# Tile 1's cross attention moved into the waits of tile 0's chain: scores in its own half of `y`, low parts on GpSimd

## The chip, the cores and the metric

The kernel runs on one core of one Trainium2 chip. The metric is the device time of one execution in microseconds (us), the median of several runs. Times inside the program come from one profiled execution and count from its first instruction.

## The reference, cut to what matters

One decoder layer over 256 tokens of 1024 channels, in float32: self attention (dilated and block-sparse), then cross attention to 256 memory rows, then the PEER expert layer, then a last norm. The change lies in the cross attention; what follows it is the expert layer.

```
x = x + cross_attention(rmsnorm(x), rmsnorm(mem))   # 4 heads of 128 channels
    lg = q @ k.T / sqrt(128); p = softmax(lg); o = p @ v; return o @ w_o
x = x + peer(rmsnorm(x))                            # 8 heads, per token:
    q = h @ w_q; sc = q @ sub_keys.T                # 2 x 128 key scores a head
    top 16 of each side, top 16 of the sums -> 16 experts and softmax gates
    y = sum over 128 experts of gate * gelu(u[e] . h) * v[e]
y = rmsnorm(x)
```

## The kernel before, in words

The 256 tokens are two tiles of 128 (`t` = 0 and 1). Every engine has its own instruction stream in an order that is written out by hand; semaphores join the streams. A matmul product goes into one of four PSUM banks `ps` in turn. `product_order` lists the products; the place in that list gives the bank (place modulo 4) and the counts that engines wait for, so the product that is four places behind waits until the first is taken out. `taken["act"]` and `taken["dve"]` count what ScalarE and VectorE have taken. The second PSUM tensor, `y` (two tiles by 1024 columns, the other four banks), collects the residual, the cross output and then the expert sum of each tile; `start_output(t, half)` puts `x` into it with an identity product.

Products in float32 quality are made of three in `fp32r`: each operand is split into a high part (a cast, on ScalarE) and a low part (value minus high part). `split_panel` does that for weight panels: ScalarE the high part, VectorE the low part. Activations of the cross output are `o_hi`, `o_lo`, those of the expert queries `h_hi`, `h_lo`.

Cross attention, tile by tile: `cross_score` (TensorE), `cross_bound` (VectorE, minimum of the negated scores), `cross_exp` (ScalarE), `cross_probs` (VectorE, normalises), `cross_turn` (TensorE transposes) and its copy (ScalarE), `cross_attend` (TensorE, two heads `i` at a time), `take_cross_o` (ScalarE, high part), `cross_o_low` (VectorE, low part), `cross_output` (TensorE, 24 products of 128x512 into `y`). Then for each tile `gained_rows` (VectorE, times the gain), `turn_rows` (TensorE), high and low part of the turned rows, `query_product` of head 0, `query_turn`, `query_scores`, and on VectorE `route_first`, which finds the first 16 experts of tile 0. Before the change tile 1's scores, exponentials and normalisations stand between tile 0's steps in all four streams.

The expert layer is 256 gathers ("slots"): 16 units (8 heads x 2 tiles) of 16 experts a token. Each is an indirect DMA of 128 rows of 8 KB, issued by GpSimd (`issue`, L1756) into one of 16 buffers (11 at first). The first waits for the first eight experts of tile 0; the second (`OWN_PLACE_OVER`) also for the last product of `cross_output(1)`; the sixth for `gained_rows(1)`; others for tile 1's query products; from the twelfth on for a buffer that TensorE has given back (`slot_free`). VectorE makes the dot product of a slot (L1644), ScalarE gelu, weight and a diagonal matrix, TensorE adds the row into `y` (L851).

SyncE loads the weight panels, 1 MB each. After `qpeer1` its stream waits until `cross_o1_1` (tile 1, heads 2 and 3) is produced; only then it loads `qpeer7` into a buffer over the cross attention's tensors, and behind it `qpeer3` and `qpeer4`.

Of the kernel before, what the change touches and what calls it, by code (L numbers as in the profile page):

```python
# [7 lines left out]
ALU = mybir.AluOpType  # L8
# [6 lines left out]
P = 128  # L15
D = 1024
S = 256
# [139 lines left out]
def product_order():  # L157
# [57 lines left out]
    def turned_rows(t):  # L215
        for half in range(2):
            if t == 0:
                add(f"cross_probs_t{half}_1", "act")
            add(f"turn{t}_{half}", "both")
# [49 lines left out]
def build(nc, x_in, mem_in, rel_bias, panels, keys_in, experts, gain_cols, gain_rows, ident_in,  # L269
          onehot_in, mask_in, iota_in, out):  # L270
    with ExitStack() as ctx:
# [191 lines left out]
        c_exp_ready = sem("c_exp_ready")  # L463
# [48 lines left out]
        def merged(c):  # L512

            return gates[:, c:c + 2, :]

# [70 lines left out]
        def _(pe):  # L586
# [156 lines left out]
            def cross_score(h, t):  # L743

                b = begin(f"cross_score{h}_{t}")
                pe.matmul(b[:, 0:S], qcT[:, h, t * P:(t + 1) * P], ckT[:, h, :],
                          start=True, stop=True).then_inc(product_ready, 1)

# [9 lines left out]

            def cross_attend(i, t):

                b = begin(f"cross_o{i}_{t}")
                all_taken(f"cross_probs_t{i}_{t}")
                for k in range(2):
                    for m in range(TILES):
                        mm = pe.matmul(b[:, k * P:(k + 1) * P], cV[:, m, (2 * i + k) * P:(2 * i + k + 1) * P],
                                       c_probsT[:, i, k * S + m * P:k * S + (m + 1) * P],
                                       start=(m == 0), stop=(m == TILES - 1))
                mm.then_inc(product_ready, 1)
# [12 lines left out]
            cross_score(2, 1)  # L781
            cross_score(3, 1)

            def cross_output(t):

                for j in range(2):
                    w_high, w_low = panel(f"ocross{j}")
                    dst = y[:, t, j * 512:(j + 1) * 512]
                    for k in range(CROSS_HEADS):
                        if j == 0 and k % 2 == 0:  # L790
                            all_taken(f"cross_o{k // 2}_{t}")
                        o_high, o_low = cut(o, slice(None), k, slice(t * P, (t + 1) * P))
# [6 lines left out]
            def turn_rows(t):  # L799

                for half in range(2):
                    if t == 0:
                        cross_turn(half, 1)
# [5 lines left out]
                    mm.then_inc(product_ready, 1)  # L809

# [104 lines left out]
        def _(act):  # L915
# [150 lines left out]
            def cross_exp(h, t):  # L1066

                b = take(f"cross_score{h}_{t}")
                act.wait_ge(c_neg_ready, t * CROSS_HEADS + h + 1)
                took(nc.scalar.activation(c_probs[:, h, t * S:(t + 1) * S], b[:, 0:S], ACT.Exp,  # L1070
                                          bias=c_neg[:, h, t:t + 1], scale=-1.0, accum_out=c_sum[:, h, t:t + 1]))
# [32 lines left out]
            def turned_rows(t):  # L1104

                for half in range(2):
                    b = take(f"turn{t}_{half}")
                    nc.scalar.copy(h_hi[:, 4 * half:4 * half + 4, t * P:(t + 1) * P],
                                   b.rearrange("p (k c) -> p k c", k=4)).then_inc(high_ready, 1)
# [14 lines left out]
            for half in range(2):  # L1124
# [74 lines left out]
            turned_rows(1)  # L1199
# [69 lines left out]
        def _(dve):  # L1269
# [134 lines left out]
            def cross_bound(h, t):  # L1404

                b = take(f"cross_score{h}_{t}")
                nc.vector.tensor_reduce(c_neg[:, h, t:t + 1], b[:, 0:S], AX.X, ALU.min).then_inc(c_neg_ready, 1)

            def cross_probs(h, t):

                dve.wait_ge(taken["act"], taken_count(f"cross_score{h}_{t}"))
# [6 lines left out]
            def cross_o_low(i, t):  # L1418

                b = take(f"cross_o{i}_{t}")  # L1420
                dve.wait_ge(high_ready, high_count(f"cross_o{i}_{t}"))
# [19 lines left out]
            for h in range(1, CROSS_HEADS):  # L1441
                cross_probs(h, 1)
# [457 lines left out]
```

## Time and profile before

| | us |
|---|---|
| median of 3 runs | 964.17 (963.46 to 964.51) |
| the profiled execution's own time | 961.84 |
| its span, first to last instruction | 960.0 |

The span is what the rows below divide up. The profiled execution is 2.3 us below the median of the runs, so differences in the span are carried over to the median as they are. TensorE is busy for 84% of the span, VectorE 65%, ScalarE 43%, GpSimd 36%; the GpSimd queue's gathers carry 268.45 MB of the 324.88 MB that the DMA engines move.

### The profile page before, as it was taken

What the parts mean: (1) busy time and instruction counts of PE and PEld (TensorE: products, weight loads), DVE (VectorE), ACT (ScalarE), POOL (GpSimd) and SP (SyncE); (2) the same over time, 40 slices, a digit from 0 to 9 for tenths busy, and PEclk for the clock granted to TensorE, in tenths of its full rate; (3) what the DMA queues carried; (4) which work ended last, traced back from release to release, by engine and by line L of the source; (5) the groups of instructions that cost most, each with busy time, mean ns of one, the idle gap of its engine ahead of it and who ended that gap; (6) DMA issues with size and microseconds to landing.
All of it is one profiled execution on the core that took longest, in us unless ns stands there. A gap on an engine that the chain in (4) does not pass through costs nothing.

```text
span 960.0 us, 11578 instructions
## 1 busy us (share of the span) xinstructions
PE 808.6 (84%) x3620; PEld 506.1 (53%) x3620; DVE 620.0 (65%) x1446; ACT 410.4 (43%) x1006; POOL 347.5 (36%) x301
## 2 busy tenths in 40 slices
PE   5999999999997899998987777777777777776776
PEld 5999998799976545553553232222222222222232
DVE  5433686465557786878777666676666766665554
ACT  5444565543564456434534324233242432424243
POOL 0000065040003455556546434444444444444410
PEclk9999999999999999999999999999999999999989
DMA  6998433257316999999999999999999999999994
GB/s 248 269 213 209 172 131 132 89 220 280 138 44 235 417 419 422 421 422 421 421 421 421 423 421 422 421 422 423 421 422 422 422 422 422 422 423 420 422 423 203
DMA packets 48803, 324.88 MB, mean 338 GB/s; under 512 B 5508, under 2 KB 8824, under 8 KB 10104
## 3 DMA queue, kind: packets, MB, share of 16 engines
q0 software_dynamic: 36864, 268.45, 67.3%
q1 hardware_dynamic: 11752, 55.61, 17.4%
q8 instruction: 25, 0.41, 0.2%
q10 hardware_dynamic: 144, 0.26, 0.1%
q14 instruction: 18, 0.15, 0.0%
HBM read 322.77 MB, written 1.54 MB: 338 GB/s over the span
## 4 chain that ended last, share of the span: by engine, by line
DMA 47%; PE 35%; DVE 6%; ACT 5%; issue 5%; POOL 1%; DVEq 0%; SPq 0%; ACTq 0%; POOLq 0%
DMA late_ring<-in_experts,expert 44%; PE y L851 8%; PE ps L603 7%; PE ps L604 7%; PE ps L605 7%; DMA arena<-in_experts,expert 2%; DVE w_lo L1284 2%; ACT w_hi L928 1%; ACT diag L1155 1%; PE ps L703 1%; POOL late_ring L1756 1%; ACT acts L1148 1%; PE ps L691 1%; DMA raw<-in_panels 1%; PE ps L681 1%
## 5 line engine op out<-in xcount | busy, mean ns | idle before, releaser
L851 PE MATMUL y<-late_ring,diag 128*128 128x512 f32 x504 | 238.7, 608 | 64.8 <-ACT diag L1155 64.8
L851 PE MATMUL y<-arena,diag 128*128 128x512 f32 x504 | 236.8, 605 | 59.7 <-ACT diag L1155 59.7
L1756 POOL DMA_INDIRECT arena<-in_experts,expert x127 | 154.4, 1216 | 231.9 <-PE y L851 117.7
L1644 DVE CUSTOM_DVE_ANT_0 arena<-arena 128x1024 f32<-128x1024 f32 x127 | 155.5, 1225 | 99.5 <-DMA arena<-in_experts,expert 99.1
L1644 DVE CUSTOM_DVE_ANT_0 late_ring<-late_ring,arena 128x1024 f32<-128x1024 f32 x129 | 157.9, 1224 | 88.8 <-DMA late_ring<-in_experts,expert 88.3
L1756 POOL DMA_INDIRECT late_ring<-in_experts,expert x129 | 150.2, 1164 | 165.8 <-PE y L851 139.9
L851 PEld LDWEIGHTS y<-late_ring,diag 128*128 128x128 f32 x504 | 91.8, 191 | 199.6 <-ACT diag L1155 105.8
L851 PEld LDWEIGHTS y<-arena,diag 128*128 128x128 f32 x504 | 92.1, 191 | 194.6 <-ACT diag L1155 99.1
L1140 ACT ACTIVATE acts<-dots 128x2 f32<-128x2 f32 x126 | 25.6, 203 | 335.1 <-DVE dots L1644 335.1
L1284 DVE TENSOR_TENSOR w_lo<-raw,w_hi 128x2048 fp32r<-128x2048 f32 x40 | 94.0, 2353 | 77.3 <-ACT w_hi L928 77.3
L603 PE MATMUL ps<-h_hi,w_hi 128*128 128x256 f32 x400 | 116.8, 292 | 1.7 <-DVE h_lo L1316 1.7
L604 PE MATMUL ps<-h_lo,w_hi 128*128 128x256 f32 x400 | 113.8, 284 | 0.0
L605 PE MATMUL ps<-h_hi,w_lo 128*128 128x256 f32 x400 | 113.7, 284 | 0.0
L928 ACT CAST w_hi<-raw 128x2048 fp32r<-128x2048 f32 x40 | 76.2, 1904 | 50.3 <-DMA raw<-in_panels 33.4
L1155 ACT ACTIVATE diag<-ident,acts 128x128 f32<-128x128 f32 x252 | 87.4, 394 | 12.1 <-PE y L851 3.1
L603 PEld LDWEIGHTS ps<-h_hi,w_hi 128*128 128x128 f32 x400 | 77.3, 193 | 5.6 <-issue 3.2
L604 PEld LDWEIGHTS ps<-h_lo,w_hi 128*128 128x128 f32 x400 | 77.4, 194 | 1.2 <-issue 1.2
L605 PEld LDWEIGHTS ps<-h_hi,w_lo 128*128 128x128 f32 x400 | 77.4, 193 | 0.0
L1736 POOL TENSOR_SCALAR arena<-arena,row_inv 128x128 f32<-128x128 f32 (+3 forms) x24 | 25.7, 1085 | 137.1 <-DVE row_inv L1338 136.8
L1148 ACT ACTIVATE acts<-acts,gate 128x1 f32<-128x1 f32 x252 | 60.5, 287 | 4.1
L603 PE MATMUL ps<-w_hi,h_hi 128*128 128x256 f32 x160 | 46.9, 293 | 2.1 <-DVE h_lo L1457 1.3
L604 PE MATMUL ps<-w_lo,h_hi 128*128 128x256 f32 x160 | 46.1, 288 | 0.0
(238 smaller groups left out, 992.5 us busy)
## 6 DMA issues: line engine op xcount, KB each, us to landing
raw<-in_panels SPq DMA_DIRECT2D x41, 1024.0 KB, 5.0
arena<-in_panels SPq DMA_DIRECT2D x5, 1024.0 KB, 6.7
arena<-line_scratch SPq DMA_DIRECT2D x8, 320.0 KB, 10.0
late_ring<-in_experts,expert POOLq DMA_INDIRECT x129, 31.7
arena<-in_experts,expert POOLq DMA_INDIRECT x127, 31.7
x<-in_x SPq DMA_DIRECT2D x2, 512.0 KB, 3.9
arena<-in_mem SPq DMA_DIRECT2D x1, 1024.0 KB, 7.3
out<-x SPq DMA_DIRECT2D x3, 256.0 KB, 7.1
```

Source lines behind the costliest of these rows:

```text
L603: pe.matmul(dst, stationary[0], moving[0], start=first, stop=False)
L604: pe.matmul(dst, stationary[0], moving[1], start=False, stop=False)
L605: return pe.matmul(dst, stationary[1], moving[0], start=False, stop=last)
L851: mm = pe.matmul(y[:, t, half * 512:(half + 1) * 512], diag[:, s % DIAGS, :], row[:, at:at + 512], start=False, stop=False, skip_group_che ...
L928: nc.scalar.copy(split_parts(n)[0], raw_panel(n)).then_inc(w_hi_ready, 1)
L1140: nc.scalar.activation(acts[:, g * GROUP:(g + 1) * GROUP], dots[:, g * GROUP:(g + 1) * GROUP], ACT.Gelu).then_inc(acts_ready, 1)
L1148: i = nc.scalar.activation(acts[:, s:s + 1], acts[:, s:s + 1], ACT.Copy, scale=gate_now[:, s:s + 1])
L1155: i = nc.scalar.activation(diag[:, s % DIAGS, :], ident[:], ACT.Copy, scale=acts[:, s:s + 1])
L1284: nc.vector.tensor_tensor(low, raw_panel(n), high.bitcast(F32), ALU.subtract).then_inc(w_lo_ready, 1)
L1644: i = nc.vector.tensor_tensor_reduce(row, row, h_rows[:, t, :], 1.0, 0.0, ALU.mult, ALU.add, dots[:, s:s + 1])
L1736: i = nc.gpsimd.tensor_scalar(pr, pr, row_inv[:, r, t:t + 1], None, ALU.mult)
L1756: nc.gpsimd.indirect_dma_start(out=slot(u, s), out_offset=None, in_=experts, in_offset=bass.IndirectOffsetOnAxis(ap=expert[:, parity, s:s ...
```

## The change

Tile 1's four score products are written straight into `y[:, 1]` (its own two banks, empty at this point) instead of `ps`. Two of them go ahead of tile 0's scores, two between tile 0's probability transposes; `start_output(0, 0)` moves behind tile 0's scores. Their minimum is taken by two VectorE instructions of two heads each, behind tile 0's low parts; their four exponentials stand on ScalarE behind `take_cross_o` of tile 0; the four normalisations stand on VectorE between the halves of tile 0's `gained_rows`. Tile 1's transposes are moved behind tile 0's turned rows, on ScalarE behind both turned halves and both squares; its heads are attended between `query_product(0, 0)`, `query_turn` and `query_scores` of tile 0. ScalarE now copies each pair of tile 1's attended heads twice (high part, and a plain copy into SBUF), and GpSimd makes the low part from the two. `cross_output(1)` waits for these, and so does the first gather.

```
     for h in range(CROSS_HEADS):
         add(f"cross_score{h}_0", "act")
-    add("cross_score0_1", "act")
     for i in range(2):
         add(f"cross_probs_t{i}_0", "act")
-    add("cross_o0_0", "both")
-    add("cross_score1_1", "act")
-    add("cross_o1_0", "both")
-    add("cross_score2_1", "act")
-    add("cross_score3_1", "act")
+    for i in range(2):
+        add(f"cross_o{i}_0", "both")
...
     cross_output(0)
     turned_rows(0)
-    add("cross_o0_1", "both")
     add("qpeer0_0", "act")
-    add("cross_o1_1", "both")
     add("qturn0_0", "act")
+    add("cross_o0_1", "act")
     add("key_score0_0", "act")
+    add("cross_o1_1", "act")
     cross_output(1)
...
-            start_output(0, 0)
+            all_taken("qcross0")
+            late_score(0)
+            late_score(1)
             all_taken("qcross1")
             for h in range(CROSS_HEADS):
-                cross_score(h, 0)
+                cross_score(h)
+            start_output(0, 0)
             start_output(0, 1)
-            cross_score(0, 1)
             cross_turn(0, 0)
+            late_score(2)
+            late_score(3)
             cross_turn(1, 0)
             cross_attend(0, 0)
-            cross_score(1, 1)
             cross_attend(1, 0)
-            cross_score(2, 1)
-            cross_score(3, 1)
...
             cross_output(0)
             turn_rows(0)
-            cross_attend(0, 1)
+            query_product(0, 0)
+            b = begin("cross_o0_1")
+            all_taken("cross_probs_t0_1")
+            cross_head(b, 0, 0)
+            query_turn(0, 0)
+            cross_head(b, 0, 1).then_inc(product_ready, 1)
+            query_scores(0, 0)
+            cross_attend(1, 1)
+            pe.wait_ge(late_exp_ready, CROSS_HEADS)
             start_output(1, 0)
-            query_product(0, 0)
-            cross_attend(1, 1)
-            query_turn(0, 0)
             start_output(1, 1)
-            query_scores(0, 0)
             cross_output(1)
...
             for h in range(CROSS_HEADS):
-                cross_exp(h, 0)
-            cross_exp(0, 1)
-            take_cross_turn(0, 0)
-            take_cross_turn(1, 0)
-            cross_exp(1, 1)
-            take_cross_o(0, 0)
-            take_cross_o(1, 0)
-            cross_exp(2, 1)
-            cross_exp(3, 1)
+                b = take(f"cross_score{h}_0")
+                act.wait_ge(c_neg_ready, h + 1)
+                took(cross_exp(h, 0, b[:, 0:S]))
+            for i in range(2):
+                take_cross_turn(i, 0)
+            for i in range(2):
+                take_cross_o(i, 0)
+            for h in range(CROSS_HEADS):
+                act.wait_ge(c_neg_ready, CROSS_HEADS + h // 2 + 1)
+                cross_exp(h, 1, late_scores(h, 1)).then_inc(late_exp_ready, 1)
             load_sqrt_table()
...
-            for half in range(2):
-                take_cross_turn(half, 1)
-                rows_square(0, half)
-            turned_rows(0)
-            take_cross_o(0, 1)
+            rows_square(0, 0)
+            turned_half(0, 0)
+            turned_half(0, 1)
+            rows_square(0, 1)
+            for i in range(2):
+                take_cross_turn(i, 1)
             rows_root(0)
             split_panel(PANELS.index("qpeer1"))
...
             take_query_tile(0, 0)
-            take_cross_o(1, 1)
             take_turned_query(0, 0)
+            late_o_high(0)
             take_scores_tile(0, 0)
+            late_o_high(1)
             scale_rows(0)
...
-            gained_rows(0)
+            gained_half(0, 0)
+            for h in range(CROSS_HEADS):
+                cross_probs(h, 1)
+            gained_half(0, 1)
             turned_rows(0)
-            cross_o_low(0, 1)
             rows_mean(0)
             rows_rstd(0)
             split_panel(PANELS.index("qpeer1"))
-            cross_o_low(1, 1)
...
+            for i in range(2):
+                pool.wait_ge(taken["act"], taken_count(f"cross_o{i}_1"))
+                pool.wait_ge(late_o_out, i + 1)
+                nc.gpsimd.tensor_tensor(o_lo[:, 2 * i:2 * i + 2, P:S], late_o(i),
+                                        o_hi[:, 2 * i:2 * i + 2, P:S].bitcast(F32), ALU.subtract
+                                        ).then_inc(late_o_ready, 1)
```

New helpers that these lines call:

```
        def late_scores(h, n):
            return y[:, 1, h * S:(h + n) * S]
            def late_score(h):
                pe.matmul(late_scores(h, 1), qcT[:, h, P:S], ckT[:, h, :],
                          start=True, stop=True).then_inc(late_scores_ready, 1)
            def late_o_high(i):
                b = take(f"cross_o{i}_1")[:, 0:S].rearrange("p (k c) -> p k c", k=2)
                nc.scalar.copy(o_hi[:, 2 * i:2 * i + 2, P:S], b).then_inc(late_o_out, 1)
                took(nc.scalar.copy(late_o(i), b))
            def late_bound(i):
                dve.wait_ge(late_scores_ready, 2 * i + 2)
                nc.vector.tensor_reduce(c_neg[:, 2 * i:2 * i + 2, 1], late_scores(2 * i, 2).rearrange(
                    "p (h m) -> p h m", h=2), AX.X, ALU.min).then_inc(c_neg_ready, 1)
```

## Rows read from the trace of the kernel before

**Rows 1.** Windows: stretch, length, busy us by engine, granted clock, DMA share, GB/s.

```profile
293.50:301.00 7.50, 7.33 (x39) 6.29 (x40) 5.20 (x37) 3.42 (x3) 0.00 (x0) 1.00 0.98 415
301.00:305.00 4.00, 1.78 (x15) 1.58 (x14) 3.66 (x10) 0.37 (x1) 1.51 (x2) 1.00 0.01 2
400.00:944.00 544.00, 425.76 (x1054) 181.01 (x1052) 367.87 (x952) 203.75 (x629) 251.78 (x215) 0.99 1.01 422
```

**Rows 2.** GpSimd's timeline: start, length, instruction; in brackets the idle time before it.

```profile
303.18 1.24 POOL L1756 DMA_INDIRECT arena<-in_experts,expert  x1 [86.54 <-DVE expert L1620]
...
338.08 0.94 POOL L1756 DMA_INDIRECT arena<-in_experts,expert  x1 [3.38 <-PE y L851]
```

**Rows 3.** SyncE's timeline, the load behind `cross_o1_1`.

```profile
291.97 0.33 SPq L555 DMA_DIRECT2D arena<-in_panels  x1
```

**Rows 4.** TensorE's timeline, tile 0's attention and its first output product.

```profile
273.41 0.63 PE L755 MATMUL ps<-ident,arena 128*128 128x128 f32 x4 [0.96 <-DVE arena L1415]
...
275.44 1.05 PE L765 MATMUL ps<-arena 128*128 128x128 f32 x8
...
277.91 0.58 PE L794 MATMUL y<-w_hi,o_hi 128*128 128x512 f32 x1
```

**Rows 5.** ScalarE's timeline in the same stretch, and its table load.

```profile
276.16 0.47 ACT L1070 ACTIVATE arena<-ps,c_neg 128x256 f32<-128x256 f32 x1 [1.50 <-DVE c_neg L1407]
...
276.62 0.64 ACT L1081 CAST o_hi<-ps 128x256 fp32r<-128x256 f32 x2
...
279.64 1.28 ACT L964 ACT_TABLE_LOAD   x1
```

**Rows 6.** VectorE's timeline: low parts, two of the normalisations, the second gained half.

```profile
277.08 0.76 DVE L1423 TENSOR_TENSOR o_lo<-ps,o_hi 128x256 fp32r<-128x256 f32 x2 [1.02 <-ACT o_hi L1081]
...
279.53 0.35 DVE L1415 TENSOR_SCALAR arena<-arena,c_inv 128x256 f32<-128x256 f32 x1
...
279.99 0.35 DVE L1415 TENSOR_SCALAR arena<-arena,c_inv 128x256 f32<-128x256 f32 x1
...
283.84 0.69 DVE L1449 TENSOR_TENSOR arena<-y,arena 128x512 f32<-128x512 f32 x1 [2.04 <-PE y L796]
```

**Rows 7.** TensorE's timeline from tile 0's turned rows to its key scores.

```profile
283.64 0.60 PE L755 MATMUL ps<-ident,arena 128*128 128x128 f32 x4
...
287.94 0.36 PE L603 MATMUL ps<-w_hi,h_hi 128*128 128x256 f32 x1 [0.63 <-DVE h_lo L1457]
...
290.89 1.05 PE L765 MATMUL ps<-arena 128*128 128x128 f32 x8
...
293.67 0.68 PE L835 MATMUL ps<-keysT,qpT 128*128 128x128 f32 x4 [0.66 <-DVE o_lo L1423]
```

**Rows 8.** ScalarE's timeline in that stretch: turned rows, the high part of `qpeer1`.

```profile
286.39 1.09 ACT L1108 CAST h_hi<-ps 128x512 fp32r<-128x512 f32 x2
...
288.98 1.89 ACT L928 CAST w_hi<-raw 128x2048 fp32r<-128x2048 f32 x1
```

**Rows 9.** VectorE's timeline: low part of `qpeer1`, start of `route_first`, first experts.

```profile
290.90 2.29 DVE L1284 TENSOR_TENSOR w_lo<-raw,w_hi 128x2048 fp32r<-128x2048 f32 x1 [1.63 <-ACT w_hi L928]
...
294.90 0.30 DVE L1586 MAX8 ranked<-arena 128x8 f32<-128x128 f32 x1 [1.37 <-ACT arena L1175]
...
302.72 0.17 DVE L1620 CAST expert<-expert_f 128x8 uint32<-128x8 f32 x1
```

**Rows 10.** VectorE's timeline earlier, a weight split while GpSimd computes.

```profile
212.07 3.42 DVE L1284 TENSOR_TENSOR w_lo<-raw,w_hi 128x2048 fp32r<-128x2048 f32 x1 [3.87 <-ACT w_hi L928]
```

**Rows 11.** GpSimd's groups by shape: busy us, mean ns of one.

```profile
L1751 POOL TENSOR_TENSOR o_lo<-arena,o_hi 128x512 fp32r<-128x512 f32 x4 | 7.1, 1808 | 0.0
```

**Rows 12.** TensorE's longest pause in this stage, its timeline.

```profile
306.15 0.41 PE L827 MATMUL ps<-ident,qpT 128*128 128x128 f32 x2 [3.37 <-DVE arena L1449]
```

**Rows 13.** Windows of the granted clock, before and after that pause; columns as in Rows 1.

```profile
273.40:277.90 4.50, 3.85 (x26) 3.17 (x27) 1.24 (x4) 2.22 (x7) 0.00 (x0) 1.00 0.00 0
308.00:314.00 6.00, 5.29 (x25) 4.92 (x24) 2.86 (x8) 3.56 (x9) 4.76 (x5) 0.50 0.98 380
```

More of the change, by code:

```diff
@@ L216, in turned_rows @@
         for half in range(2):
+            add(f"turn{t}_{half}", "both")
             if t == 0:
                 add(f"cross_probs_t{half}_1", "act")
-            add(f"turn{t}_{half}", "both")
     def query(h, t):
@@ L462, in build @@
         c_neg_ready = sem("c_neg_ready")
-        c_exp_ready = sem("c_exp_ready")
+        late_scores_ready = sem("late_scores_ready")
+        late_exp_ready = sem("late_exp_ready")
+        late_o_out = sem("late_o_out")
+        late_o_ready = sem("late_o_ready")
         c_inv_ready = sem("c_inv_ready")
@@ L757, in cross_turn, with cross_head @@
                 mm.then_inc(product_ready, 1)
+            def cross_head(b, i, k):
+                for m in range(TILES):
+                    mm = pe.matmul(b[:, k * P:(k + 1) * P], cV[:, m, (2 * i + k) * P:(2 * i + k + 1) * P],
+                                   c_probsT[:, i, k * S + m * P:k * S + (m + 1) * P],
+                                   start=(m == 0), stop=(m == TILES - 1))
+                return mm
             def cross_attend(i, t):
@@ L762, in cross_attend @@
                 all_taken(f"cross_probs_t{i}_{t}")
[L763 to L768, printed above, removed]
-            start_output(0, 0)
+                cross_head(b, i, 0)
+                cross_head(b, i, 1).then_inc(product_ready, 1)
+            all_taken("qcross0")
+            late_score(0)
+            late_score(1)
             all_taken("qcross1")
             for h in range(CROSS_HEADS):
-                cross_score(h, 0)
+                cross_score(h)
+            start_output(0, 0)
             start_output(0, 1)
-            cross_score(0, 1)
             cross_turn(0, 0)
+            late_score(2)
+            late_score(3)
             cross_turn(1, 0)
             cross_attend(0, 0)
-            cross_score(1, 1)
             cross_attend(1, 0)
-            cross_score(2, 1)
-            cross_score(3, 1)
             def cross_output(t):
@@ L809, in turn_rows @@
                     mm.then_inc(product_ready, 1)
+                    if t == 0:
+                        cross_turn(half, 1)
             def query_product(h, t):
@@ L1064, in _, with cross_exp @@
             take_queries(1)
[L1066 to L1071, printed above, removed]
+            def cross_exp(h, t, b):
+                return nc.scalar.activation(c_probs[:, h, t * S:(t + 1) * S], b, ACT.Exp,
+                                            bias=c_neg[:, h, t:t + 1], scale=-1.0, accum_out=c_sum[:, h, t:t + 1])
             def take_cross_turn(i, t):
@@ L1102, in rows_square, with turned_half @@
                                      ).then_inc(ffn_sq_ready, 1)
-            def turned_rows(t):
-                for half in range(2):
-                    b = take(f"turn{t}_{half}")
-                    nc.scalar.copy(h_hi[:, 4 * half:4 * half + 4, t * P:(t + 1) * P],
-                                   b.rearrange("p (k c) -> p k c", k=4)).then_inc(high_ready, 1)
+            def turned_half(t, half):
+                b = take(f"turn{t}_{half}")
+                nc.scalar.copy(h_hi[:, 4 * half:4 * half + 4, t * P:(t + 1) * P],
+                               b.rearrange("p (k c) -> p k c", k=4)).then_inc(high_ready, 1)
             def rows_root(t):
@@ L1122, in scale_rows @@
                                      ).then_inc(h_rows_ready, 1)
-            for half in range(2):
-                take_cross_turn(half, 1)
-                rows_square(0, half)
-            turned_rows(0)
-            take_cross_o(0, 1)
+            rows_square(0, 0)
[4 more added lines that the diff above has]
+                take_cross_turn(i, 1)
             rows_root(0)
@@ L1198, in _ @@
             take_scores_tile(1, 0)
-            turned_rows(1)
+            for half in range(2):
+                turned_half(1, half)
             rows_root(1)
@@ L1667, in _ @@
             route_first()
-            gained_rows(1)
+            for half in range(2):
+                gained_half(1, half)
             split_panel(PANELS.index("qpeer2"))
@@ L1753, in _ @@
                                         ).then_inc(merged_ready, 1)
+            for i in range(2):
+                pool.wait_ge(taken["act"], taken_count(f"cross_o{i}_1"))
[3 more added lines that the diff above has]
+                                        ).then_inc(late_o_ready, 1)
             def issue(u, s, parity):
```

65 lines of the change are left out of this document (32 added, 33 removed).

## The prediction

> **What bounds the kernel now.** I read the windows first. From 400 to 944 us the DMA engines are fully busy at 422 GB/s; a gather is 128 rows of 8 KB, 1.05 MB, so one takes 2.49 us and 256 of them 636 us. Ahead of that lies a hole: from 293.50 to 301.00 three weight panels load at 415 GB/s, then for 4.00 us the DMA engines move 2 GB/s [rows 1]. The hole ends when the first gather's data starts to flow, about 1.8 us after its issue at 303.18, and that issue had waited for VectorE's first experts [rows 2]. So the end of the kernel is the start of the gathers plus a fixed transfer time. The busy shares mislead: TensorE's 84% decides nothing behind 305 us. What decides is the serial chain that leads to 303.18, and I walked it backwards in the four engines' timelines, looking in each step for tile 1's work standing between two of tile 0's.
>
> The chain has three places with such work. (1) Tile 0's attended heads are ready on TensorE, but ScalarE sits in tile 1's exponential, which itself waited 1.50 us for a minimum on VectorE; the high parts start only at 276.62 [rows 5], the low parts at 277.08 [rows 6], the first output product at 277.91 [rows 4]. (2) From 283.64 to 287.94 TensorE has tile 1's transposes ahead of tile 0's rows, and ScalarE puts two copies and two squares ahead of the turned rows' high parts, which start at 286.39 [rows 7, 8]. (3) From 287.94 to 294.90, where `route_first` begins, the query product is followed by tile 1's attention at 290.89, and the key scores wait until 293.67 for a bank that VectorE frees with tile 1's low part, behind the split of `qpeer1` [rows 7, 9].
>
> **The change, place by place.** Up to 273.41, where tile 0's second pair of transposes starts [rows 4], nothing moves: two late scores replace one `start_output` in front of the scores (two products of 256 columns for one of 512), and tile 0's minima, exponentials and normalisations wait on each other, not on tile 1's minimum that went. The other two late scores fit into the 0.96 us for which TensorE waits there [rows 4].
>
> Place 1. Transposes at 273.41 are ready 0.63 later [rows 4], ScalarE's copy takes 0.6 more (as one of the two casts of 128x512 in [rows 8]), so the second pair is attended from 274.73 and ready 1.05 later, 275.78. The first pair, attended from 273.85, has its high part at 275.3 and its low part at 275.75, each about 0.4 [rows 5, 6]. The first output product starts at 275.8 instead of 277.91. The second pair's low part is there at 276.65, needed six products later, at 277.2. Gain 2.1.
>
> Place 2. The output's products take 283.64 - 277.91 = 5.7 [rows 4, 7], so tile 0's first turned rows are issued at 281.5. Ready after 0.6, high part 0.6, low part 0.7 (the 128x512 of [rows 6]), and TensorE starts the query product at 283.6 with 0.15 of semaphore time. Before: 287.94 [rows 7]. Gain of this place 2.2, sum 4.3. Two covers must hold. ScalarE has tile 1's four exponentials (0.47 each, behind two minima of about 0.6 each: 277.3 to 279.2) and the table load of 1.28 with its dummy (to 280.8) and a square of 0.6 (to 281.4) [rows 5]; the turned rows come at 282.1, so 0.7 is free. VectorE has four normalisations of 0.46 (the distance of the two in [rows 6]) behind the first gained half, 279.5 to 281.4; the second gained half can start at 283.84 - 2.1 = 281.7 [rows 6], so 0.3 is free. If that cover is gone, what is late next is the second turned half, which the query product needs only 12 products in, so a few tenths more cost nothing.
>
> Place 3. The query product takes 290.89 - 287.94 = 2.95 [rows 7] and is ready at 286.7. ScalarE is not: after the second high part (283.6) come a square of 0.6, two copies of 0.5 and the root (285.3), and then the high part of `qpeer1`, 1.89 [rows 8], of which the next instruction waits 1.8. The query is copied at 287.1, not 286.7: 0.4 lost. Copy 0.37, transpose 0.4, copy 0.37, with 0.1 between each: key scores start at 288.5, the bank being free. From key scores to `route_first` it is 294.90 - 293.67 = 1.23 [rows 7, 9], so `route_first` starts at 289.75. VectorE's split of `qpeer1` follows ScalarE's at 287.2 and takes 2.29 [rows 9]: done at 289.5, just in time. The one head of tile 1 between the transposes is 0.44 on TensorE, which waits there anyway; the two extra ScalarE copies (0.3 each) fit between 288.45 and 289.2, where ScalarE would wait for the key scores. Gain of this place 0.8.
>
> Sum: 2.1 + 2.2 + 0.8 = 5.1, that is 294.90 to 289.75. `route_first` itself is unchanged (294.90 to the experts at 302.72 [rows 9]), so the first gather is issued at 298.0 and its data flows at 299.85.
>
> **What must come along.** The panels: SyncE's load at 291.97 waits for `cross_o1_1` [rows 3]. Attended from 288.95, that is ready at 290.0, so the loads run 1.8 earlier, to 299.2 [rows 1], 0.6 before the gathers. Were they later, their rest would only share the DMA engines, microsecond for microsecond; this caps the gain at 4.0 + 1.8 = 5.8. The low parts on GpSimd: 128x512 took 1.81 [rows 11], so 128x256 about 0.9; the second runs from 290.6 to 291.5. `cross_output(1)` starts at 291.6 (attention, then two `start_output` of 0.87) and needs it at 293.0; its 5.7 end at 297.3. The second gather waits for this and is wanted by 300.5. The first gather's new wait is over at 291.5. Behind that, tile 1's rows follow `route_first` on VectorE and so move by the same 5. If they did not: the sixteenth gather, issued at 338.08 [rows 2], has 15 gathers of 2.49 ahead of it, 305.0 + 37.3 = 342.3 at the least, and needs 1.8; that leaves 2.4, so an unmoved tile 1 would take back 2.7 at most.
>
> The price that the trace doesn't show is what GpSimd's subtraction does to VectorE in the selection. Bounds: nothing, or what a split lost while GpSimd computed, 3.42 - 2.29 = 1.13 [rows 9, 10]. Twice that is the upper end, 2.3. I take nothing: the splits have two tensors in SBUF, the instructions at 289.5 to 291.5 (maxima, replacements, index searches on 128x128) have one. A gain below zero cost can't come from here. The Trainium skill, page "SBUF — State Buffer", section "SBUF: two separate sides", says that a VectorE instruction with two SBUF inputs and a GpSimd one exclude each other for a whole instruction, and whoever came first holds the ports. The 3.42 agrees with it. By that rule the split of `qpeer1` holds the first subtraction until 289.5 and the second ends before the first sum of pairs in `route_first`, so the sum stays 5.1.
>
> **Rivals.** (a) GpSimd holds VectorE. For: [rows 10]. Against: the form of the instructions. One hit of 1.13 gives 4.0, two give 2.8: 960.2 to 961.4. (b) The panel loads do not move, because something keeps `cross_o1_1` at 291.8; then they end at 301.0, 1.15 after the gathers want to start, and the gain is 4.0: 960.2. Against: nothing of tile 1 but its copied transposes is in its way. (c) Slower: TensorE's clock falls inside the chain. After its pause of 3.37 us the granted clock was 0.50, that is 1.2 GHz, from 308 to 314 [rows 12, 13]. Tile 0's output (5.7) and query product (2.95) at that level cost 8.7 more, against 5.1 gained: 3.6 slower, 967.8. It decides from 5.1 us of matmul time at the low level. Against: with 3.85 of 4.50 busy and a pause of 0.96 the clock stayed at 1.00 [rows 4, 13], and the new order has no pause over 1 us in the chain. (d) The second gather waits for tile 1's output: it takes over 3.2 us of lateness (297.3 to 300.5) before it costs, 8.3 before all is lost. Then the time is that of before, 964.2.
>
> **How the numbers follow.** All differences are of the profiled span (960.0, its execution 961.84); the median of the runs, 964.17, is taken to move by the same amount: 964.17 - 5.15 = 959.0. Chances: forecast (gain 4.4 to 6) 0.72, (a) 0.12, (b) 0.07, (c) 0.04, (d) or another pace that takes nearly all back 0.05. The range goes down to the cap of 5.8 with 0.4 of scatter of the runs, 957.9, and up to one hit of (a) or (b) with the same scatter and something of a second, 960.9. What a measurement can tell from no change is 0.2%, 1.9 us: faster 0.91, same 0.05, slower 0.04.
>
> **What would show it.** First output product near 275.8, query product near 283.6, `route_first` near 289.7, first gather near 298.0; panel loads ending just before the gathers' data; DMA share 1.0 from there on, without a hole near 300 or 320 to 335. An exponential or table load directly ahead of the turned rows' high parts would break place 2; a longer split of `qpeer1` or longer maxima beside GpSimd's two subtractions would be (a). The prediction is wrong if the gathers start earlier by 5 and the end doesn't follow.

## The result, and the profile after

| | before | after |
|---|---|---|
| median of 5 runs, us | 963.46 (960.74 to 964.51) | 957.20 (956.54 to 959.27) |
| span of the profiled execution | 960.0 | 955.3 |

The ratio is 0.994, with a 95% interval of 0.9921 to 0.9958: the change is faster, by 6 us on these runs. The profiled spans differ by 4.7, of which 0.3 lies ahead of the changed stage (269.22 and 268.89 in the table below). The forecast was 959.0 in a range of 957.9 to 960.9, so the median lies 0.7 below the range. The chain is almost where it was foretold; what was off is told behind the experiments.

TensorE's timeline of the changed kernel, with the lines that answer to [rows 4] and [rows 7] (start, length, instruction, idle time before it):

```profile
273.08 0.63 PE L767 MATMUL ps<-ident,arena 128*128 128x128 f32 x4
273.54 2.01 PE L774 MATMUL ps<-arena 128*128 128x128 f32 x16
275.68 0.47 PE L813 MATMUL y<-w_hi,o_hi 128*128 128x512 f32 x1
...
281.28 0.60 PE L825 MATMUL ps<-ident,arena 128*128 128x128 f32 x4
...
283.44 0.36 PE L610 MATMUL ps<-w_hi,h_hi 128*128 128x256 f32 x1
...
286.39 0.60 PE L774 MATMUL ps<-arena 128*128 128x128 f32 x4
287.38 0.41 PE L846 MATMUL ps<-ident,qpT 128*128 128x128 f32 x2 [0.39 <-ACT qpT L1191]
...
288.30 0.68 PE L854 MATMUL ps<-keysT,qpT 128*128 128x128 f32 x4
```

Both pairs of heads now run in one piece (x16), and the first output product follows 2.6 us behind the start of tile 0's second pair of transposes, where it was 4.5. The first turned rows follow the output's last product directly (L825 at 281.28), and the key scores have no wait for a bank.

ScalarE's timeline, answering to [rows 5] and [rows 8]:

```profile
275.60 0.37 ACT L1102 CAST o_hi<-ps 128x256 fp32r<-128x256 f32 x1 [0.58 <-PE ps L774]
277.13 0.48 ACT L1091 ACTIVATE arena<-y,c_neg 128x256 f32<-128x256 f32 x1 [1.16 <-DVE c_neg L1442]
...
279.08 1.28 ACT L987 ACT_TABLE_LOAD   x1
...
281.91 0.59 ACT L1135 CAST h_hi<-ps 128x512 fp32r<-128x512 f32 x1 [0.76 <-PE ps L825]
...
285.09 1.92 ACT L951 CAST w_hi<-raw 128x2048 fp32r<-128x2048 f32 x1
286.88 0.40 ACT L1191 COPY qpT<-ps 128x256 f32<-128x256 f32 x1
```

Tile 1's exponential again waits over a microsecond for its minimum, but nothing of tile 0 stands behind it any more. The turned rows find ScalarE idle for 0.76 us: the cover of place 2 held. The query's copy has no idle time ahead of it: it came straight from the split of `qpeer1`, as foretold.

VectorE's timeline, answering to [rows 6] and [rows 9]:

```profile
276.07 0.42 DVE L1462 TENSOR_TENSOR o_lo<-ps,o_hi 128x256 fp32r<-128x256 f32 x1 [0.54 <-ACT o_hi L1102]
...
281.48 0.69 DVE L1482 TENSOR_TENSOR arena<-y,arena 128x512 f32<-128x512 f32 x1 [0.20 <-PE y L815]
...
287.04 2.29 DVE L1314 TENSOR_TENSOR w_lo<-raw,w_hi 128x2048 fp32r<-128x2048 f32 x1 [1.62 <-ACT w_hi L951]
289.53 0.30 DVE L1620 MAX8 ranked<-arena 128x8 f32<-128x128 f32 x1 [0.19 <-ACT arena L1203]
...
297.35 0.17 DVE L1654 CAST expert<-expert_f 128x8 uint32<-128x8 f32 x1
```

Here the covers (the time that VectorE still waits when the work put in front is done) were as thin as estimated, 0.20 us at the second gained half and 0.19 at `route_first`. The selection from 289.53 to 297.35 takes 7.82, exactly as before (294.90 to 302.72, [rows 9]), with both GpSimd subtractions near it. In the two kernels of the experiments that have no such subtraction it takes 7.82 and 7.80. So the price that I had put between 0 and 2.3 is 0, and the subtractions took 0.92 and 0.73:

```profile
289.00 0.92 POOL L1793 TENSOR_TENSOR o_lo<-arena,o_hi 128x256 fp32r<-128x256 f32 x1 [72.69 <-ACT arena L1109]
290.64 0.73 POOL L1793 TENSOR_TENSOR o_lo<-arena,o_hi 128x256 fp32r<-128x256 f32 x1 [0.72 <-ACT arena L1109]
298.45 1.21 POOL L1798 DMA_INDIRECT arena<-in_experts,expert  x1 [7.08 <-DVE expert L1654]
```

That is GpSimd's timeline, answering to [rows 2]. Its last line holds a surprise: the gather starts 1.10 us behind the start of the experts' line on VectorE, 298.45 - 297.35. Before, it was 0.46, 303.18 - 302.72 [rows 2, 9]. SyncE's load, answering to [rows 3], and the windows (stretch, length, busy us by engine, granted clock, DMA share, GB/s), answering to [rows 1]:

```profile
289.90 0.33 SPq L562 DMA_DIRECT2D arena<-in_panels  x1
```

```profile
291.50:299.10 7.60, 7.60 (x43) 6.53 (x42) 6.68 (x35) 2.01 (x2) 0.65 (x1) 1.00 0.97 405
299.10:300.30 1.20, 0.93 (x8) 0.72 (x7) 1.17 (x4) 0.24 (x1) 0.90 (x2) 1.00 0.02 7
308.00:314.00 6.00, 5.71 (x47) 5.31 (x46) 5.25 (x16) 2.86 (x7) 5.09 (x4) 1.00 1.01 419
400.00:940.00 540.00, 423.80 (x1040) 180.63 (x1039) 364.51 (x947) 200.07 (x621) 253.50 (x213) 0.98 1.01 422
```

The hole of 4.00 us ahead of the gathers has shrunk to 1.2, the rate behind it is the same 422 GB/s, and TensorE's clock, at 0.50 from 308 to 314 before [rows 13], is at 1.00 there. That is not where the gain comes from: from the first gather to the end it is 656.8 us with the low clock and 656.9 without it (next table).

### The profile page after: what moved, and what is told of

It is laid out like the page before. It is cut to its first block, busy times and chain, and to the rows that moved or that the text cites. A ratio compares the mean times of both kernels' runs of the same rounds, so it can differ in the third digit from the quotient of the medians.

```text
span 955.3 us, 11577 instructions
## 1 busy us (share of the span) xinstructions
PE 810.4 (85%) x3620; PEld 506.7 (53%) x3620; DVE 619.5 (65%) x1442; ACT 411.5 (43%) x1008; POOL 359.5 (38%) x303
## 4 chain that ended last, share of the span: by engine, by line
DMA 47%; PE 39%; issue 5%; ACT 4%; DVE 3%; POOL 1%; DVEq 0%; SPq 0%; ACTq 0%; POOLq 0%
DMA late_ring<-in_experts,expert 44%; PE y L870 9%; PE ps L610 8%; PE ps L611 8%; PE ps L612 8%; DMA arena<-in_experts,expert 2%; ACT diag L1183 1%; POOL late_ring L1798 1%; PE ps L710 1%; PE ps L698 1%; ACT acts L1176 1%; DMA raw<-in_panels 1%; DVE w_lo L1314 1%; PE ps L688 1%; ACT w_hi L951 1%
## 5 line engine op out<-in xcount | busy, mean ns | idle before, releaser
L870 PE MATMUL y<-late_ring,diag 128*128 128x512 f32 x504 | 241.2, 614 | 63.5 <-ACT diag L1183 63.5
L870 PE MATMUL y<-arena,diag 128*128 128x512 f32 x504 | 239.5, 611 | 58.9 <-ACT diag L1183 58.9
L1798 POOL DMA_INDIRECT late_ring<-in_experts,expert x129 | 155.0, 1202 | 161.3 <-PE y L870 135.4
L1798 POOL DMA_INDIRECT arena<-in_experts,expert x127 | 156.5, 1233 | 150.0 <-PE y L870 111.2
L1771 POOL TENSOR_SCALAR arena<-arena,row_inv 128x128 f32<-128x128 f32 (+3 forms) x24 | 29.1, 1227 | 133.4 <-DVE row_inv L1368 133.2
```

The costliest lines, as they stand in the source:

```text
L870: mm = pe.matmul(y[:, t, half * 512:(half + 1) * 512], diag[:, s % DIAGS, :], row[:, at:at + 512], start=False, stop=False, skip_group_che ...
L1771: i = nc.gpsimd.tensor_scalar(pr, pr, row_inv[:, r, t:t + 1], None, ALU.mult)
L1798: nc.gpsimd.indirect_dma_start(out=slot(u, s), out_offset=None, in_=experts, in_offset=bass.IndirectOffsetOnAxis(ap=expert[:, parity, s:s ...
```

## The experiments

All ratios are against the kernel before, from 6 to 12 executions of each kernel (5 in the row "after"). The runs e1 to e4, e5 to e8, and e9 with e10 are three comparisons, each with its own executions of the kernel before (25, 29 and 11); the changed kernel itself was timed only for the result and in e1. The table puts the profiled executions side by side. "Stage start" is the start of tile 0's first minimum, the first VectorE instruction behind the weight splits. Ahead of it the kernels differ in TensorE's first instructions for this stage, which cost the same (0.87 us of one `start_output` before, 0.86 of two late scores after), and e9 in the place of one panel load. "Experts" is the start of VectorE's last instruction for the first eight experts. All in us.

| kernel | stage start | from it to `route_first` | experts to first gather | first gather to end | span | ratio (95%) |
|---|---|---|---|---|---|---|
| before | 269.22 | 25.68 | 0.46 | 656.8 | 960.0 | 1 |
| after | 268.89 | 20.64 | 1.10 | 656.9 | 955.3 | 0.9940 (0.9921 to 0.9958) |
| e1 after again | 267.34 | 20.66 | 1.10 | 656.7 | 953.6 | 0.9951 (0.9938 to 0.9963) |
| e2 scores only | 269.22 | 23.63 | 0.46 | 656.8 | 957.9 | 0.9984 (0.9971 to 0.9996) |
| e3 rows behind | 270.59 | 22.45 | 1.10 | 656.7 | 958.7 | 0.9968 (0.9953 to 0.9982) |
| e4 low on VectorE | 270.28 | 21.85 | 0.46 | 657.2 | 957.6 | 0.9967 (0.9953 to 0.9980) |
| e5 wait apart | 269.59 | 20.64 | 0.47 | 657.0 | 955.5 | 0.9948 (0.9931 to 0.9964) |
| e6 delay ahead | 271.18 | 23.77 | 1.10 | 657.5 | 961.7 | 0.9996 (0.9981 to 1.0011) |
| e7 delay behind | 269.21 | 20.67 | 1.10 | 657.8 | 956.6 | 0.9974 (0.9962 to 0.9987) |
| e8 loads late | 269.12 | 20.66 | 1.11 | 662.8 | 961.5 | 1.0008 (0.9994 to 1.0021) |
| e9 apart, loads | 269.00 | 20.63 | 0.46 | 657.1 | 955.0 | 0.9951 (0.9935 to 0.9968) |
| e10 apart, once more | 271.50 | 20.63 | 0.46 | 656.5 | 956.9 | 0.9939 (0.9921 to 0.9957) |

### The changed kernel again

No edit. 

> The changed kernel once more, for its size and its scatter. Theory (the end follows the first gather one for one): first output product of tile 0 about 2.1 us, route_first about 5.1 us earlier than in the profile of before, the first gather 4.7 to 5.2 earlier, ratio 0.9940 to 0.9955. Rival (part of the 6.3 us between the two medians is not in this chain but in the scatter of executions): the ratio stays below 0.9940 only if the runs of before scatter upward again, and the profiled chain still shows about 5.

Ratio 0.9951: 4.7 us (5.3 between the medians), where the first comparison had 5.8 by its ratio and 6.3 between its medians. The first gather, counted from the stage start, is 4.4 us earlier than before, not the expected 4.7 to 5.2. The rival is borne out: part of the 6.3 was scatter of executions, and the profiled chain to `route_first` still shows 5.0. The median of the kernel before was 963.24 here, from 25 executions between 960.26 and 965.83. The chain repeated itself to 0.02 us (20.64 and 20.66), while the stage start moved by 1.55. So the gain of the change is stable, and the scatter that these profiles show comes from ahead of the stage. VectorE's timeline shows where. Before the change, the start of the weight split near 128 us and of the first minimum:

```profile
128.41 2.29 DVE L1284 TENSOR_TENSOR w_lo<-raw,w_hi 128x2048 fp32r<-128x2048 f32 x1
```

```profile
269.22 0.42 DVE L1407 TENSOR_REDUCE c_neg<-ps 128x1 f32<-128x256 f32 x1 [0.23 <-PE ps L746]
```

The same two instructions in this run:

```profile
126.51 2.29 DVE L1314 TENSOR_TENSOR w_lo<-raw,w_hi 128x2048 fp32r<-128x2048 f32 x1
```

```profile
267.34 0.42 DVE L1437 TENSOR_REDUCE c_neg<-ps 128x1 f32<-128x256 f32 x1
```

1.90 us early at 128 us, 1.88 early at the stage start: in this pair the difference was complete in the first 129 us, and nothing was added in the 140 us behind. Up to there the splits wait for weight panels (at 105.87 ScalarE's half of one waited 3.67 us for its load in this run). In the run with a delay ahead of `route_first` (below) that split starts at 130.37, 1.96 late, and the stage start is 1.96 late. In eleven of the twelve profiles the distance between the two instructions is 140.8 to 141.0 us; in the first profile of the changed kernel it is 140.0 (128.91 to 268.89).

### Place 1 alone

```
 kernel: as after, but
                 for half in range(2):
+                    if t == 0:
+                        cross_turn(half, 1)
                     b = begin(f"turn{t}_{half}")
...
-                    if t == 0:
-                        cross_turn(half, 1)
...
             cross_output(0)
             turn_rows(0)
-            query_product(0, 0)
-            b = begin("cross_o0_1")
-            all_taken("cross_probs_t0_1")
-            cross_head(b, 0, 0)
-            query_turn(0, 0)
-            cross_head(b, 0, 1).then_inc(product_ready, 1)
-            query_scores(0, 0)
-            cross_attend(1, 1)
+            cross_attend(0, 1)
             pe.wait_ge(late_exp_ready, CROSS_HEADS)
             start_output(1, 0)
+            query_product(0, 0)
+            cross_attend(1, 1)
+            query_turn(0, 0)
             start_output(1, 1)
+            query_scores(0, 0)
 ScalarE: copies, squares, high parts in the order of before
 VectorE: cross_o_low(0, 1) and cross_o_low(1, 1) where they were
 GpSimd: no subtractions
```

> Only the scores, exponentials and normalisations of tile 1 moved (place 1 of the prediction); transposes, attention and low parts where they were, low parts on VectorE. Theory: 2.1 us of gain, all of it there when tile 0's first output product starts, the rest of the chain as long as before: ratio 0.9978. Rival (the places are not additive, what place 1 gives is taken back by a later wait): the query product of tile 0 starts at the time of before, ratio 0.999 to 1.000.

From stage start to `route_first` 23.63 instead of 25.68: 2.05 of gain, all kept. TensorE's timeline has the query product here:

```profile
285.89 0.36 PE L610 MATMUL ps<-w_hi,h_hi 128*128 128x256 f32 x1 [0.62 <-DVE h_lo L1483]
```

at the same stage start (269.22) as before, where it was at 287.94 [rows 7]. The ratio, 0.9984, gives 1.5, with an interval from 0.4 to 2.8. The rival, a time of 0.999 to 1.000, is not excluded by the ratio alone; its sign in the profile, a query product at the time of before, is absent.

### Place 2 undone

```
-            rows_square(0, 0)
-            turned_half(0, 0)
-            turned_half(0, 1)
-            rows_square(0, 1)
-            for i in range(2):
-                take_cross_turn(i, 1)
+            for half in range(2):
+                take_cross_turn(half, 1)
+                rows_square(0, half)
+            for half in range(2):
+                turned_half(0, half)
 TensorE and product_order: cross_turn(half, 1) ahead of each turned half
```

> The changed kernel with place 2 undone: tile 1's transposes ahead of tile 0's turned rows on TensorE, two copies and both squares ahead of the high parts on ScalarE. Theory: 2.2 us of the gain go, first gather about 2.2 later than in the changed kernel, ratio about 0.997. Rival (these instructions lie in waits of ScalarE either way): first gather within 0.5 us of the changed kernel's, ratio 0.9945.

`route_first` comes at 22.45 instead of 20.64, 1.8 later; the ratio 0.9968 is 1.6 us above the changed kernel's. ScalarE's timeline shows the queue that was put back:

```profile
283.63 0.59 ACT L1097 COPY arena<-ps 128x512 f32<-128x512 f32 x1 [1.36 <-PE ps L767]
284.11 0.60 ACT L1128 ACTIVATE x<-y 128x512 f32<-128x512 f32 x1
...
284.69 0.59 ACT L1097 COPY arena<-ps 128x512 f32<-128x512 f32 x1
285.16 0.62 ACT L1128 ACTIVATE x<-y 128x512 f32<-128x512 f32 x1
...
285.74 1.09 ACT L1135 CAST h_hi<-ps 128x512 fp32r<-128x512 f32 x2
```

The query product is 2.15 later than in the changed kernel (16.70 behind the stage start against 14.55), the key scores only 1.81 (21.22 against 19.41). Most of the missing 0.34 is the time for which the query's copy waits behind ScalarE's half of the split of `qpeer1` in the changed kernel (it starts 3.44 behind the query product's start, here 3.14): places 2 and 3 are not quite additive. The rival, a first gather within 0.5 us, is out: it came 1.8 later, counted from the stage start.

### Low parts back on VectorE

```
-                nc.scalar.copy(o_hi[:, 2 * i:2 * i + 2, P:S], b).then_inc(late_o_out, 1)
-                took(nc.scalar.copy(late_o(i), b))
+                nc.scalar.copy(o_hi[:, 2 * i:2 * i + 2, P:S], b).then_inc(high_ready, 1)
...
             split_panel(PANELS.index("qpeer1"))
+            cross_o_low(0, 1)
+            cross_o_low(1, 1)
...
 GpSimd: no subtractions, no wait for them
```

> The changed kernel with tile 1's low parts on VectorE again, between the low part of qpeer1 and route_first, and without the second copies on ScalarE and the two subtractions on GpSimd. Theory: the second low part is ready only at about 290.3 and holds route_first to 290.7 instead of 289.5: 1.2 us of the gain go, ratio about 0.9955 to 0.9965. Rival (GpSimd's subtractions and the doubled copies cost what they save): no loss, ratio 0.9945 or lower.

VectorE's timeline:

```profile
290.65 0.42 DVE L1459 TENSOR_TENSOR o_lo<-ps,o_hi 128x256 fp32r<-128x256 f32 x1
291.79 0.42 DVE L1459 TENSOR_TENSOR o_lo<-ps,o_hi 128x256 fp32r<-128x256 f32 x1 [0.72 <-ACT o_hi L1106]
292.13 0.28 DVE L1619 MAX8 ranked<-arena 128x8 f32<-128x128 f32 x1
```

The second low part waits for ScalarE and holds `route_first` back by 1.21 (21.85 against 20.64), as expected. But the first gather follows the experts by 0.46 again, so only 0.6 of the 1.2 reaches it. Moving the low parts to GpSimd is worth 1.2 at `route_first`, and its form costs 0.64. Counted from the stage start the profile ends 0.9 to 1.0 later than the two of the changed kernel; the ratio, 0.9967, lies just above what was expected and can't tell 0.6 from 1.2.

### The first gather's wait apart

```
                     if n == 0:
-                        pool.wait_ge(late_o_ready, 2)
+                        wait_apart(pool, late_o_ready, 2)     # the wait on an instruction of its own
                         pool.wait_ge(first_experts_ready, 1)
```

> The changed kernel with one edit: the first gather's new wait for the low parts gets an instruction of its own ahead of it, so that the gather itself holds only the wait for the first experts, as before the change. Seen so far: from the experts on VectorE to the first gather on GpSimd 0.46 us in the three kernels without the new wait and 1.10 in the three with it. Theory (the wait for the experts stands in an instruction of its own when the gather has two waits, and the gather's start-up follows it): 0.46 again, first gather and end 0.6 earlier, ratio 0.9944 where the changed kernel has 0.9951. Rival (GpSimd pays this because it has computed shortly before): 1.10 stays, ratio 0.9951.

GpSimd's timeline, with the experts on VectorE at 298.03:

```profile
291.34 0.73 POOL L1793 TENSOR_TENSOR o_lo<-arena,o_hi 128x256 fp32r<-128x256 f32 x1 [0.72 <-ACT arena L1109]
298.50 1.25 POOL L1798 DMA_INDIRECT arena<-in_experts,expert  x1 [6.42 <-DVE expert L1654]
```

0.47, with GpSimd's subtractions still there: it is the form of the wait, not that GpSimd has computed. The trace has a separate semaphore instruction in both kernels. In the changed one it holds the wait for the experts and stands 0.9 us ahead of the gather, which itself holds the wait for the low parts, long over; here it is the other way round: the separate instruction, for the low parts, stands 6.4 us ahead of the gather. The same came out in two further runs, 0.46 each. Counted from the stage start, the three profiled executions with the wait apart end after 685.9, 686.0 and 685.4, the two of the changed kernel after 686.4 and 686.3. The ratios (0.9948, 0.9951, 0.9939) don't separate them from 0.9951 and 0.9940: the timed runs cannot show half a microsecond. That the 0.64 reaches the end rests on these five profiles alone.

### A delay ahead of `route_first`, and one behind it

```
+            for n in range(3):
+                nc.vector.tensor_reduce(idle[:, n:n + 1], g_ffn_row, AX.X, ALU.max)
             route_first()
```

and the same lines behind `route_first()`.

> The changed kernel with three VectorE reductions of 128x1024 (about 1.1 us each, results unused) ahead of route_first. Theory (the first gather sets the end): first gather, and with it tile 1's chain, 3.3 us later, the time 3.3 longer, ratio 0.9985. Rival (something else paces the end, the first gather has slack): less than 1 us longer, ratio at most 0.996.

> The changed kernel with the same three reductions behind route_first, ahead of tile 1's gained rows: tile 1's chain is 3.3 us later, the first gather is not. Theory (the DMA engines have gathers in hand when tile 1's chain returns the first buffers; before the change the smallest reserve was 2.4 us at the least): nothing to 1 us longer, ratio 0.995 to 0.996, the DMA share stays at 1.0. Rival (tile 1's chain on TensorE sets the end, as the chain of waits draws it up to about 380 us): 3.3 longer, ratio 0.9985.

VectorE's timeline of the first, then of the second:

```profile
291.57 3.46 DVE L1703 TENSOR_REDUCE idle<-arena 128x1 f32<-128x1024 f32 x3
294.95 0.28 DVE L1621 MAX8 ranked<-arena 128x8 f32<-128x128 f32 x1
```

```profile
299.69 3.46 DVE L1704 TENSOR_REDUCE idle<-arena 128x1 f32<-128x1024 f32 x3
```

The delay ahead makes `route_first` 3.13 later and the ratio 0.9996 instead of 0.9951, 4.3 us longer. Counted from the stage start the profile ends 4.1 to 4.2 later (690.5 against 686.4 and 686.3): 3.1 by the delay, 0.3 in the selection (8.15 instead of 7.82), and 0.6 to 0.8 behind the first gather (657.5 instead of 656.7 to 656.9). All of the delay arrives; why the two other parts came is open. The low clock that came back in this run (0.50 from 306.2 to 310, after a pause of TensorE of 4.20 us) does not account for the last part: before the change it was as low, with 656.8 to the end. The delay behind leaves the first gather where it was, and from there to the end it is 657.8 instead of 656.7 to 656.9, 1.0 longer in the profile, the theory's upper end. The ratio says 0.9974, 2.2 longer, between the theory and the rival's 3.3; the DMA share did not stay at 1.0, as the theory had it. The windows of the second show what the stretch at full DMA rate loses:

```profile
310.00:330.00 20.00, 17.36 (x98) 12.64 (x97) 17.45 (x59) 8.78 (x24) 9.54 (x7) 1.00 1.01 423
...
335.00:345.00 10.00, 10.00 (x40) 5.88 (x40) 7.91 (x29) 3.91 (x10) 5.47 (x4) 0.95 0.98 380
```

380 GB/s instead of 422 over 10 us is 1.0 us of transfer. The sixteenth gather is issued 37.7 us behind the first, where it was 32.1 and 33.0 in the two profiles of the changed kernel and 34.9 before [rows 2]. So it came 4.7 to 5.6 us later than in the changed kernel, more than the delay itself. By the prediction's reckoning the 15 gathers ahead of it are 37.3 us of transfer, so they ran out 0.4 us before its data could flow. That leaves 0.6 of the 1.0 without an account. Whether the timed executions lose another microsecond is open: the intervals of 0.9974 and 0.9951 (0.9962 to 0.9987, 0.9938 to 0.9963) still touch.

### The panels' loads held

```
-                    last_use = "cross_o1_1" if early == "qpeer7" else f"probs_t{SELF_HEADS - 1}"
+                    last_use = "ocross1_1" if early == "qpeer7" else f"probs_t{SELF_HEADS - 1}"
```

> The changed kernel with the three weight panels' loads held until the last product of tile 1's cross output (about 297 instead of 290 us). Theory (what of them falls behind the gathers' start shares the DMA engines microsecond for microsecond): the loads run from about 299 to 306.5, some 6 us of them beside gathers, the time about 6 longer, ratio 1.001. Rival (the gathers' first microseconds do not need the full rate): less than 2 us longer, ratio at most 0.997.

SyncE's timeline, then the windows:

```profile
297.45 0.33 SPq L562 DMA_DIRECT2D arena<-in_panels  x1
```

```profile
290.00:297.00 7.00, 7.00 (x29) 5.05 (x28) 5.86 (x38) 3.60 (x4) 0.91 (x2) 1.00 0.00 0
300.00:305.00 5.00, 2.45 (x19) 1.86 (x18) 4.12 (x5) 3.24 (x9) 4.17 (x3) 1.00 1.01 423
```

Nothing moves from 290 to 297, then gathers and panels share a full rate. The first gather is issued at the same distance from the stage start, and the end is 6.0 later (662.8 against 656.8). By the ratios it is 5.5. The loads were held 7.3 us (28.3 behind the stage start instead of 21.0), and in the changed kernel their last packet lay 1.0 us ahead of the gathers' first; so 6.3 us of them should fall beside gathers, and 6.0 arrive at the end. The panel loads are thus a second bound just beneath the chain, microsecond for microsecond.

### Loads earlier, with the wait apart

```
-EARLY_BEHIND = {..., "kv2": "qpeer2", "qpeer1": "qpeer7"}
+EARLY_BEHIND = {..., "kv2": "qpeer2", "qpeer3": "qpeer7"}
```

> The first gather's wait apart, as in the run before, and the load of qpeer3 moved ahead of SyncE's wait for cross_o1_1, so that only two of the three panels load between that wait and the gathers. Seen so far: with the wait apart, the third panel's last packet lies 0.1 us ahead of the gathers' first. Theory (the panels just miss the gathers): the hole ahead of the gathers is 2.5 us longer, first gather and end as with the wait apart alone, within 0.3 us, ratio 0.9945 to 0.9950. Rival (the panels' tail already holds the first gather back in some executions): 0.5 us or more on top, ratio 0.9940 or lower.

> The wait apart once more, on the chip of the run with the loads moved. Theory: experts to first gather 0.46 to 0.47 us again, ratio 0.9945 to 0.9950. Rival (the 0.64 us seen once was chance): 1.1 us in this profile.

The last panel packet now lies 2.95 us ahead of the gathers' first, where it was 0.1 and 0.6 in the two runs with the wait apart alone, and the time is the same (the profiles end 686.0 us behind the stage start, and 685.9 and 685.4). The panels had just missed. "Experts to first gather" is 0.46 in both, as expected; the ratio of the repeat, 0.9939, lies just below its expected 0.9945 to 0.9950, well within its interval. By this, a further cut of the chain would need the loads in this place to reach the end; that was not run.

## Why the prediction was right or wrong

**Right: what bounds the kernel.** From the first gather to the end it is 656.5 to 657.5 us in ten of the twelve executions, whatever was done ahead. The two exceptions are those in which the transfers themselves were disturbed, by late buffers and by late panels.

**Right: the chain.** Counted from the stage start, the first output product came 1.9 earlier (2.1 foretold), the query product 4.2 (4.3), the key scores and `route_first` 5.0 (5.1). The 0.9 that is gained between the query product and `route_first` is place 3 (0.8 foretold); it was not undone by itself. Place 1 alone gave 2.05. Undoing place 2 cost 1.8 of the 2.2: the rest is mostly hidden by the split of `qpeer1`, as place 3 had it with its 0.4. The low parts, the panels' start (289.90) and the second gather did not get in the way. Rivals (a), (c) and (d) did not occur: the selection kept its length, the granted clock was 1.00 from 267 to 291 us, and the second gather followed the first after 0.30 us of issue, with no wait. (b) did not occur either, but the panels' end is a real bound, shown by the held loads, that was missed by 1.0 us.

**Wrong: the last step.** The prediction had "the median of the runs, 964.17, is taken to move by the same amount: 964.17 - 5.15 = 959.0", with "0.4 of scatter of the runs". Two terms of this sum were mis-sized: the base and the scatter. Three executions within 1.05 us had been taken for the spread of the kernel. Over 65 further executions it runs from 959.9 to 966.4, and its medians were 963.24, 963.38 and 963.48; 964.17 lay 0.7 to 0.9 above them. The profile's own 961.84, 2.3 below that median, had been the sign of it. In the comparison of the result the median before was 963.46; with that base the prediction's own sum gives 958.3 and its lower end 957.3, and the measured 957.20 still lies 0.1 below. The rest is the scatter of the changed kernel, 955.55 to 959.27 over its two comparisons. The second of these, six executions, has a median of 957.98, just inside the stated range, so that the first fell outside is in part chance.

The size of the move, 5.15, was right within about a microsecond: 4.4 and 4.5 in the two profiles aligned at the stage start, 4.7 and 5.3 by ratio and medians of the second comparison, 5.8 and 6.3 by those of the first. The scatter seen in the profiles arises mostly ahead of the stage and has nothing to do with the change.

**Missed: the price of the new wait.** "The first gather's new wait is over at 291.5" was true and beside the point. The second wait put the wait for the experts onto an instruction of its own ahead of the gather, and the gather's start-up then came after it: 0.64 us in all six profiled executions with that form. So of the chain's 5.0 only 4.4 reached the gathers. This error made the gain smaller than foretold, while the measured median lay below the range: it is not what put the time outside.

## What to carry to other kernels

Where a long stretch at full DMA rate ends a kernel, as in this one, its time is the start of that stretch plus a constant; check that constant first, then work only on the chain ahead, and look for what else ends its transfers just before. In such a chain, take the other tile's work out of the in-order streams between two steps of the first, and put it where the engine waits; covers of 0.2 us were enough in a chain that repeats itself to 0.04. Align two profiles at the first instruction of the changed stage before subtracting spans, and take a base from more than three executions. Where an indirect DMA on GpSimd ends the chain, as here, let it carry the wait that ends last, and give a wait that is long over an instruction of its own; other instructions were not tried.

## What the runs showed that I had not expected

- The first indirect DMA on GpSimd starts 1.10 us behind the start of the instruction that releases it when that wait stands on an instruction of its own ahead of it, and 0.46 to 0.47 when the DMA carries it.
- The chain repeats to 0.04 us over seven profiles (20.63 to 20.67), while the 270 us ahead of it spread over 4.2 us (stage starts from 267.34 to 271.50).
- GpSimd's subtraction of 128x256 took 0.73 us, but 0.92 to 0.93 where it began 0.3 us before the end of VectorE's split of `qpeer1` (289.00; the split runs from 287.04 to 289.33). With place 2 undone it began 0.3 us behind that end (292.51 against 292.21) and took 0.73. The Trainium skill, page "SBUF — State Buffer", section "SBUF: two separate sides", has the later of two such instructions wait until the earlier is through; the 0.2 us fits that in kind, though the split had 0.3 to go. VectorE's split kept its 2.29, and the selection behind it its 7.82, beside the second subtraction.
